# Norm weight rows issued from ScalarE's queue, and the second block's lambda, angles, Sin and Exp moved from the first feed-forward into the first attention

## The reference, cut to what matters

```python
def first_block(x, mem, ...):
    for i in range(DEPTH):                       # 2
        xn = rms_norm(h, norm_mix[i])
        mn = rms_norm(mem, norm_mem[i])
        mkv = mn @ w_mem_kv[i]
        ...                                      # attention, output projection
        hn = rms_norm(h, norm_ffn[i])
        gu = hn @ w_gate_up[i]
        h = h + (jax.nn.silu(gu[..., :D_FF]) * gu[..., D_FF:]) @ w_down[i]
    return rms_norm(h, norm_final)

def _rope_tables(positions):                     # the angles, Sin
    inv_freq = 1.0 / (ROPE_THETA ** (jnp.arange(0, MLA_ROPE_DIM, 2, dtype=jnp.float32) / MLA_ROPE_DIM))
    ang = positions.astype(jnp.float32)[..., None] * inv_freq
    return jnp.cos(ang)[:, :, None, :], jnp.sin(ang)[:, :, None, :]

# lambda, in _hybrid_layer
lam = jnp.exp(jnp.sum(lf[0] * lf[1])) - jnp.exp(jnp.sum(lf[2] * lf[3])) + lam_init
```

## Time and profile before

| | |
|---|---|
| runs | 1948.5, 1946.1, 1948.7 us; median 1948.5 |
| the profiled execution | 1948.7 us, of which the span is 1946.9 us |
| PE busy | 1517.2 us, 78% |
| DVE, ACT, POOL busy | 625.5, 529.9, 134.0 us |
| mean granted TensorE clock | 0.885 |
| moved by DMA | 542 MB, of it 402.7 MB (192 x 2 MB) experts' weights |

### The profile page before, as it was taken

How to read it: one execution, slowest core, us unless ns; L and a number is a source line. 1 busy time by engine, 2 the same in 40 slices (tenths; PEclk the granted TensorE clock), 3 DMA queues, 4 the chain that set the end, 5 groups by cost and what they waited for, 6 DMA issues and landing times.

```text
span 1946.9 us, 25845 instructions
## 1 busy us (share of the span) xinstructions
PE 1517.2 (78%) x11156; PEld 1031.7 (53%) x11174; DVE 625.5 (32%) x980; ACT 529.9 (27%) x868; POOL 134.0 (7%) x151
## 2 busy tenths in 40 slices
PE   7999999999999997899888665566555566555665
PEld 7888999887999897789463111121111112111211
DVE  5665445666454544445761000000000000000000
ACT  6455443545434456425631000000000000000000
POOL 0351000031000013410200000000000000000000
PEclk9999999999999989999989777867878878778776
DMA  8443555433555443213098999999999999999997
GB/s 268 153 142 130 173 183 183 152 133 128 182 185 192 121 127 115 84 48 130 7 382 345 427 429 428 427 429 427 428 428 428 428 428 428 427 428 428 427 428 305
DMA packets 138561, 542.01 MB, mean 278 GB/s; under 512 B 10093, under 2 KB 103490, under 8 KB 113890
## 3 DMA queue, kind: packets, MB, share of 16 engines
q1 hardware_dynamic: 138418, 540.50, 70.7%
q0 software_dynamic: 48, 0.13, 0.0%
HBM read 539.56 MB, written 1.05 MB: 278 GB/s over the span
## 4 chain that ended last, share of the span: by engine, by line
PE 46%; DMA 43%; DVE 5%; ACT 3%; POOL 2%; issue 1%; SPq 0%; DVEq 0%; ACTq 0%; POOLq 0%
DMA ew<-in_expert_w_up_dram 14%; DMA ew<-in_expert_w_gate_dram 14%; DMA ew<-in_expert_w_down_dram 14%; PE bank L1082 11%; PE bank L1083 11%; PE bank L1084 11%; PE bank L1577 2%; PE bank L1600 1%; PE bank L1089 1%; DVE wL L1621 1%; POOL arena L671 1%; PE bank L1103 1%; PE bank L1166 1%; PE bank L1305 1%; ACT wH L714 1%
## 5 line engine op out<-in xcount | busy, mean ns | idle before, releaser
L1577 PE MATMUL bank<-ew,xeT 128*32 128x512 f32 x2048 | 340.2, 799 | 236.5 <-DMA ew<-in_expert_w_up_dram 128.3
L1621 DVE TENSOR_TENSOR wL<-ring,wH 128x2048 fp32r<-128x2048 f32 x128 | 294.8, 2303 | 273.5 <-ACT wH L714 273.2
L1577 PEld LDWEIGHTS bank<-ew,xeT 128*32 128x32 f32 x2048 | 64.5, 129 | 495.5 <-DMA ew<-in_expert_w_up_dram 210.4
L714 ACT ACTIVATE wH<-ring 128x2048 fp32r<-128x2048 f32 x128 | 244.4, 1910 | 286.5 <-PE bank L1084 284.1
L1082 PE MATMUL bank<-xH,wH 128*128 128x256 f32 x1056 | 303.9, 288 | 7.6 <-DVE wL L1621 7.0
L1083 PE MATMUL bank<-xL,wH 128*128 128x256 f32 x1056 | 300.2, 284 | 0.0
L1084 PE MATMUL bank<-xH,wL 128*128 128x256 f32 x1056 | 300.1, 284 | 0.0
L1600 PE MATMUL bank<-ew,tok 128*32 128x256 f32 x2048 | 173.0, 497 | 103.0 <-DMA ew<-in_expert_w_down_dram 95.4
L1082 PEld LDWEIGHTS bank<-xH,wH 128*128 128x128 f32 x1056 | 203.8, 193 | 14.3 <-issue 9.0
L1083 PEld LDWEIGHTS bank<-xL,wH 128*128 128x128 f32 x1056 | 203.9, 193 | 0.8
L1084 PEld LDWEIGHTS bank<-xH,wL 128*128 128x128 f32 x1056 | 203.8, 193 | 0.0
(11 more groups left out here) (287 smaller groups left out, 1785.3 us busy)
## 6 DMA issues: line engine op xcount, KB each, us to landing
ew<-in_expert_w_gate_dram SPq DMA_DIRECT2D x64, 2048.0 KB, 46.1
ew<-in_expert_w_up_dram SPq DMA_DIRECT2D x64, 2048.0 KB, 46.0
ew<-in_expert_w_down_dram SPq DMA_DIRECT2D x64, 2048.0 KB, 46.6
ring<-in_w_gate_up_dram SPq DMA_DIRECT2D x44, 1024.0 KB, 5.1
ring<-in_w_down_dram SPq DMA_DIRECT2D x22, 1024.0 KB, 4.9
ring<-in_w_in_dram SPq DMA_DIRECT2D x22, 1024.0 KB, 5.3
ring<-in_w_out_dram SPq DMA_DIRECT2D x12, 1024.0 KB, 4.9
ring<-in_w_in_fox_dram SPq DMA_DIRECT2D x10, 1024.0 KB, 9.6
```

The source lines that it names most:

```text
L714: act.activation(wH[:, n % 2, w], ring[:, slot(n), w], ACT.Copy).then_inc(w_hi, 1)
L1577: mm = pe.matmul(bank[half][32 * j:32 * j + 32, :], xeT[:, k, CAP * e:CAP * e + CAP], w_[:, m, 512 * j:512 * j + 512], start=(k == 0), sto ...
L1621: dve.tensor_tensor(wL[:, n % 2, w], ring[:, slot(n), w], wH[:, n % 2, w].bitcast(F32), ALU.subtract).then_inc(w_split, 1)
```

## The change

Two edits. The nine `vec` transfers leave SP's program and stand at the head of ACT's, ahead of its wait for the constants; what they move and the semaphore that they count are the same. And the second block's preparation leaves the first feed-forward: `angles` goes to the end of step 6 of the first attention on DVE, `lambda_sums` to the end of step 8, `lambda_weights` to the end of step 12; the Exp of lambda goes to step 10 on ACT; the two Sin go to the head of the second layer's attention, ahead of the `preload(ACT.Exp)` that stands there already. The reload of Silu's table goes away.

```diff
@@ sync @@
-            def vec(r, src, n):
-                sp.dma_start(vrows[r:r + n, :], src).then_inc(vec_in, 16)
-
-            vec(ROW["mix0"], norm_mix.rearrange("l (k p) -> (l k) p", p=P), 16)
...
-            vec(ROW["subln"], diff_subln, 1)
-
             load_cols(mem_u[1], MEMPROJ[1][0], MEMPROJ[1][1])
@@ scalar @@
+            def vec(r, src, n):
+                act.dma_start(vrows[r:r + n, :], src).then_inc(vec_in, 16)
+
+            vec(ROW["mix0"], norm_mix.rearrange("l (k p) -> (l k) p", p=P), 16)
...
+            vec(ROW["subln"], diff_subln, 1)
 
             act.wait_ge(consts, 6)
             squares("mem", tok, mem_in)
@@ scalar, head of a layer's attention @@
+                if L == 1:
+                    act.wait_ge(tab_v, 5)
+                    act.activation(cs[:, 0], ang[:, 0], ACT.Sin).then_inc(tab_s, 1)
+                    act.activation(cs[:, 1], ang[:, 1], ACT.Sin).then_inc(tab_s, 1)
                 preload(ACT.Exp)
@@ scalar, in a step of the attention @@
+                    if L == 0 and i == 10:
+                        act.wait_ge(lam_s, 2)
+                        act.activation(lamv[:, 2:4], lamv[:, 0:2], ACT.Exp).then_inc(lam_s, 1)
@@ scalar, feed-forward @@
-                if L == 0:
-                    act.wait_ge(lam_s, 2)
-                    act.activation(lamv[:, 2:4], lamv[:, 0:2], ACT.Exp).then_inc(lam_s, 1)
-                    act.wait_ge(tab_v, 5)
-                    act.activation(cs[:, 0], ang[:, 0], ACT.Sin).then_inc(tab_s, 1)
-                    act.activation(cs[:, 1], ang[:, 1], ACT.Sin).then_inc(tab_s, 1)
-                    preload(ACT.Silu)
@@ vector, end of a step of the attention @@
+                    if L == 0 and i == 6:
+                        angles()
+                    if L == 0 and i == 8:
+                        lambda_sums()
+                    if L == 0 and i == 12:
+                        lambda_weights()
@@ vector, feed-forward @@
-                if L == 0:
-                    lambda_sums()
-                    angles()
-                    lambda_weights()
```

More of the change, by code:

```diff
@@ L798, in exps @@
                     turned(15)
+            def vec(r, src, n):
+                act.dma_start(vrows[r:r + n, :], src).then_inc(vec_in, 16)
+            vec(ROW["mix0"], norm_mix.rearrange("l (k p) -> (l k) p", p=P), 16)
+            vec(ROW["mem0"], norm_mem.rearrange("l (k p) -> (l k) p", p=P), 16)
+            vec(ROW["ffn0"], norm_ffn.rearrange("l (k p) -> (l k) p", p=P), 16)
+            vec(ROW["attn"], attn_norm.rearrange("l (k p) -> (l k) p", p=P), 8)
+            vec(ROW["ffn2"], ffn_norm2.rearrange("l (k p) -> (l k) p", p=P), 8)
+            vec(ROW["bgate"], b_gate.rearrange("l (k p) -> (l k) p", p=P), 16)
+            vec(ROW["mlaq"], mla_q_norm.rearrange("l (k p) -> (l k) p", p=P), 2)
+            vec(ROW["mlakv"], mla_kv_norm.rearrange("l (k p) -> (l k) p", p=P), 2)
+            vec(ROW["subln"], diff_subln, 1)
             act.wait_ge(consts, 6)
```

## The result

| | before | after |
|---|---|---|
| median of 8 runs each, taken together | 1947.79 us (1945.11 to 1949.35) | 1941.21 us (1936.9 to 1942.25) |
| ratio, 95% interval | | 0.9965 [0.9954, 0.9976] |
| profiled execution, its span | 1948.7, 1946.9 | 1941.29, 1939.5 |

So the direction is right, the size is not, and a part of the size differs from one measurement to the next. Three places of the profile of after say where the 7.4 us between the two spans lie.

A forecast was written before the change was run, and what follows sets the result against it. PE's matmuls bound the kernel up to the experts, then the experts' weight transfers. Terms -2.9 (feed-forward wait) and -1.9 (start) with two zeros sum to -4.8 us: 1948.7 to 1943.9 us; 8-in-10 range 1941.8 to 1950.

The forecast's parts named there:

- The angles fit ahead of the minima: First attention, DVE: angles' 2.56 us delay step 7's minima to 105.86, hidden by 0.37 us before PE's scores at 106.23.
- The Sin is hidden: Second layer's attention, ACT: two Sin and a table load, 1.64 us, against 1.35 us idle; cost 0, at most 0.3.
- ACT is free for unit 0: Start: nine issues at SP's 3.58 us leave ACT free at 8.93, 0.9 us before unit 0's copy at 9.83.
- SP's gain: SP's own queue moves up by 3.58 us, but nothing waits for what follows, so it is worth nothing.
- A: Start: ACT's issues cost 0.7 to 0.8 us each, PE starts at 17.3; total -2.1, 1946.6 us; chance 0.24.
- C: First attention: angles hold the minima beyond 106.23, PE pays at most 2.2 us; total -2.6, 1946.1 us; chance 0.07.
- Rival B: Start: ACT's issues wait behind SP's long ones, PE starts at 25.2; total +5.8, 1954.5 us; chance 0.13.
- Rival D: Start: unit 0 may land before 9.83, gain grows by up to 0.9; total -5.7, 1943.0 us; chance 0.06.
- the first term: First feed-forward: moving lambda and angles off DVE removes PE's whole wait for `wL`, gaining 2.9 us.
- the second term: Start: nine row issues on ACT let PE's first real matmul begin at 14.69 instead of 16.57, gaining 1.9 us.
- The bound that I wrote down and left: Start: if the ninth row again took 5.13 us, PE would begin at 9.4, gaining 1.3 us.

The follow-up runs named there:

- the second pair: Kernels before and after, both unchanged, measured and profiled again: 1945.65 and 1941.85 us against 1946.75 for before beside them.
- rows_only: Kernel before with only the nine row issues moved to ACT's queue: 1946.03 us against 1947.47, ratio 0.999 [0.998, 1.0001].
- after_again: Kernel after, unchanged, run again for another profile and more times: 1941.85 us, ratio to before 0.9974 [0.9964, 0.9984].
- before_again: Kernel before, unchanged, run again for another profile and more times: 1945.65 us, ratio to before 0.9997 [0.9987, 1.0008].

## Why the prediction was wrong, point by point

**Right.** PE's wait in the feed-forward is gone, with nothing late in its place. The angles fit ahead of the minima with 0.39 us left. The Sin is hidden. ACT's nine issues cost 3.81 us, and ACT is free for unit 0 at 9.14, before it lands. Everything else of SP's gain was worth nothing, and rivals A and C didn't come.

**Rival B** fell on its own row: no ACTq row of over 1 us, the longest is 0.73. SP was held for 4.17 us on two transfers while ACT made five issues of about 0.3 us. The Trainium skill (Perfetto Trace Analysis, DMA Instruction — HWDGE) has one engine lock the unit that makes the descriptors until it is done; here, what held SP did not hold ACT. Rival D looks half true in this profile, with unit 0 0.45 us earlier, but its landing varies by more than that with the rows on either queue, and it was worth nothing, since the rows ended the start.

**Wrong, the first term: "The gain is the whole wait, 2.9 us."** The wait was priced at its own length. It measures 3.1 us where the clock stays up, and 4.6 between the profiles of before and after, since in before a stretch at 1.2 GHz follows it in full work. This is the mis-sized term: with it at 4.6 the sum would be 1.7 us lower, 1942.2 us, with the range's low end of 1941.8 just below it. The range was made from the rivals and the spread of three runs and had no clock in it. The row was there to be read in before's windows. As it comes in two of four executions it is worth about 1 us in a median, an estimate, and can be a part of why the two measurements differ; that it is all of it isn't shown. The Trainium skill (TensorE: Matmul & The Clock Gate, HAM oscillation — how this bites in real kernels) says that PE is throttled again by waits and then has to be warmed again, and names waits for DMA; the wait here is one for DVE, and did the same in two of four executions.

**Wrong, the second term: "as the new queue has no megabyte in front of the rows".** It was forecast at 1.9 us and measures 0.8 in after, 1.6 between the second pair and 0.6 in `rows_only`. Over all profiles PE's first real matmul is at 16.27 to 17.11 in the seven with the rows on SP, and at 14.82 to 15.93 in the five with them on ACT and nothing else changed at the start; the means are 1.2 us apart. The bound that I wrote down and left, 1.3 us with a landing of 5.13, was the better one; what is missing from it to 0.8 are the ninth issue's 0.14 us, the landing's 0.19 and 0.18 in the turning. The Trainium skill's rule that I set against it (DMA: Bandwidth & Descriptors, Issuing engines are not separate DMA queues) was right here: 4.4 to 5.4 us in either queue, 2.9 with unit 0 held back.

**The sum.** In the second pair both terms are near the forecast: 1.6 + 3.1 = 4.7 us by the copies up to 658 us, where 4.8 were forecast. That is luck in part, as the half clock came in neither execution and the row landed soonest in `after_again`. In the first pair the errors are larger and of opposite signs, 0.8 + 4.6 = 5.4, and 1.9 us more come from the second block. There before and `before_again`, one program, differ by another 1.5 us, so I put this down to the executions and not to the change; no run shows it.

**The base.** 4.8 us were taken from the profiled execution's 1948.7. Eight runs of before have a median of 1947.79, and in the later measurements it is 1945.40 to 1947.47. So of the 2.7 us between 1943.9 and 1941.21 the base has 0.9 and the gain 1.8. With so small a change this decides: the second measurement's 1941.85 is inside the range, by 0.05 us.

**Open** is what decides in an execution whether the clock falls behind a wait of 2.9 us; no run here controls it.

## What to carry to other kernels

A wait of the engine that bounds the kernel is not over when it ends: read the granted clock of the microseconds behind it, and price the wait with what they lose, as a chance if other executions lack it. Take the gain from a median of many runs, not from one profiled execution. Moving small loads to another engine's queue takes their issues off the first engine, but not the megabytes that were issued before them off their way; that takes another order of issue. And two profiles of one program tell what of a difference is the change's: here 2.7 us by the end of the dense part were nobody's.

## What was unexpected of the hardware

- With a wait of 2.9 us PE's granted clock fell to 0.50 in two of four executions, once while PE still stood and once when it was at work again, and cost 1.5 and 2.6 us. With 5.5 us it fell in the one profile taken and cost 2.7 us, with 1.5 us it did not fall. It did not fall there in any profile in which PE had its work or matmuls of zeros instead.
- The first matmuls of the kernel, behind 9.7 us of nothing, took 421 ns each and the later ones of the same form 275, with the granted clock shown as 1.00 in both stretches:

```profile
9.00:12.70 3.70, 3.00 (x14) 3.03 (x15) 2.08 (x4) 2.05 (x2) 0.00 (x0) 1.00 1.09 379
12.70:15.00 2.30, 2.30 (x19) 2.30 (x18) 0.91 (x1) 0.84 (x3) 0.00 (x0) 1.00 1.04 370
```

With matmuls of zeros ahead all 32 took 275 ns. So at a kernel's start the duration of a form tells more than the clock's column.
- SP's issue of `x` blocked for 4.17 us and left ACT's issues alone.
